# Two transformer blocks in one kernel: the hand-over from the first block's down projection to the linear attention of the second

## The reference, cut to what matters

```
x = x + rms_norm(f, norm_ffn_post_g)                      # f = (silu(h @ w_gate) * (h @ w_up)) @ w_down
mod = silu(c) @ w_ada + b_ada                             # sh1, sc1, g1, sh2, sc2, g2
h = rms_norm(x, norm1_g) * (1 + sc1) + sh1
gq, gk, gv, gr, glr, aq, ak, av = split(h @ w_in)         # 256, 256, 512, 512, 16, 512, 512, 512 columns
log_a = log_sigmoid(glr @ gla_w_gate + gla_b_gate) / 16
y_gla = gated linear attention of gq / 8, gk, gv, log_a   # then rms_norm, times silu(gr)
y_att = dilated attention of aq, ak, av
x = x + g1 * (concat(y_gla, y_att) @ w_out)               # then the second feed-forward
```

## Time and profile before

| | |
|---|---|
| time, median of 3 runs | 1385.92 us |
| profiled execution, its own time | 1384.31 us |
| its span, first to last instruction | 1382.6 us |
| TensorE busy | 1364.7 us |
| VectorE (DVE) busy | 873.8 us |
| ScalarE (ACT) busy | 584.9 us |
| GpSimd (POOL) busy | 57.4 us |
| mean granted clock of TensorE | 0.997 |
| DMA | 146.82 MB, 106 GB/s |

### The profile page before, as it was taken

One profiled execution on the slowest core, in us unless ns is written; L12 is line 12 of the kernel. 1 busy time (PEld: TensorE's weight loads), 2 busy tenths in 40 slices (PEclk: granted clock), 3 DMA queues, 4 the chain that ended last, 5 costly groups with the idle time before them and its releaser, 6 DMA issues.

```text
span 1382.6 us, 18985 instructions
## 1 busy us (share of the span) xinstructions
PE 1364.7 (99%) x6662; PEld 1113.0 (81%) x6662; DVE 873.8 (63%) x1473; ACT 584.9 (42%) x979; POOL 57.4 (4%) x119
## 2 busy tenths in 40 slices
PE   9999999999999999999998999999999999999999
PEld 7777777778988888888885787777798888888887
DVE  6667676678777777774336677776566656655221
ACT  5455455553453332233224534675455444443221
POOL 0000000000002121120000000000000000000000
PEclk9999999999999999999999999999999999999999
DMA  5222212214316555564431211111213232233332
GB/s 206 92 77 77 77 61 79 77 59 137 98 54 211 193 186 196 190 198 154 139 125 44 94 65 62 62 61 62 76 58 107 91 99 98 91 105 114 86 97 87
DMA packets 42615, 146.82 MB, mean 106 GB/s; under 512 B 5425, under 2 KB 5697, under 8 KB 42561
## 3 DMA queue, kind: packets, MB, share of 16 engines
q1 hardware_dynamic: 34592, 120.13, 26.7%
q0 software_dynamic: 7824, 25.70, 5.5%
q10 hardware_dynamic: 144, 0.26, 0.1%
HBM read 143.97 MB, written 2.10 MB: 106 GB/s over the span
## 4 chain that ended last, share of the span: by engine, by line
PE 92%; DVE 4%; ACT 3%; issue 1%; DMA 0%; DVEq 0%; SPq 0%; ACTq 0%
PE bank L644 61%; PE bank L846 13%; PE bank L662 4%; PE bank L785 3%; PE bank L872 2%; PE bank L962 2%; PE bank L893 1%; PE bank L911 1%; PE bank L752 1%; PE bank L1092 1%; PE bank L914 1%; DVE w_lo L1841 0%; DVE hbuf L1901 0%; ACT w_hi L1260 0%; DVE xT L2197 0%
## 5 line engine op out<-in xcount | busy, mean ns | idle before, releaser
L1841 DVE TENSOR_TENSOR w_lo<-raw,w_hi 128x1024 fp32r<-128x1024 f32 (+1 forms) x224 | 268.0, 1197 | 163.2 <-ACT w_hi L1260 158.3
L1260 ACT ACTIVATE w_hi<-raw 128x1024 fp32r<-128x1024 f32 (+1 forms) x224 | 231.6, 1035 | 285.9 <-PE bank L644 260.6
L644 PE MATMUL bank<-h_hi,w_hi 128*128 128x512 f32 x856 | 339.6, 397 | 0.7 <-DVE w_lo L1838 0.5
L644 PE MATMUL bank<-h_hi,w_lo 128*128 128x512 f32 x856 | 333.5, 390 | 0.0
L644 PE MATMUL bank<-h_lo,w_hi 128*128 128x512 f32 x856 | 333.3, 389 | 0.0
L644 PEld LDWEIGHTS bank<-h_hi,w_hi 128*128 128x128 f32 x856 | 160.7, 188 | 37.8 <-issue 3.8
L644 PEld LDWEIGHTS bank<-h_hi,w_lo 128*128 128x128 f32 x856 | 160.7, 188 | 34.0
L644 PEld LDWEIGHTS bank<-h_lo,w_hi 128*128 128x128 f32 x856 | 160.8, 188 | 33.8 <-issue 1.7
L644 PE MATMUL bank<-f_hi,w_lo 128*128 128x512 f32 x352 | 136.9, 389 | 0.0
L644 PE MATMUL bank<-f_hi,w_hi 128*128 128x512 f32 x352 | 136.9, 389 | 0.0
L644 PE MATMUL bank<-f_lo,w_hi 128*128 128x512 f32 x352 | 136.9, 389 | 0.0
(11 more groups left out here) (351 smaller groups left out, 1954.6 us busy)
## 6 DMA issues: line engine op xcount, KB each, us to landing
raw<-in_w_up SPq DMA_DIRECT2D x66, 512.0 KB, 3.3
ada<-in_w_ada POOLq DMA_DIRECT2D x96, 256.0 KB, 3.1
raw<-in_w_mix SPq DMA_DIRECT2D x47, 512.0 KB, 3.3
raw<-in_w_down SPq DMA_DIRECT2D x32, 512.0 KB, 3.5
raw<-in_w_in SPq DMA_DIRECT2D x25, 512.0 KB, 3.3
raw<-in_w_gate SPq DMA_DIRECT2D x22, 512.0 KB, 3.3
raw<-in_w_out SPq DMA_DIRECT2D x16, 512.0 KB, 3.3
raw<-in_w_down SPq DMA_DIRECT2D x16, 384.0 KB, 3.3
```

The lines of the kernel that those rows point to most:

```text
L644: last = pe.matmul(to[:, :], wt[:, slot, k, :], act_[:, rhs0 + k, :], start=(k == first and n == 0), stop=(k == K - 1 and n == 2))
L1260: act.activation(w_hi[:, s, k0:K, :], raw[:, s, k0:K, :], ACT.Copy).then_inc(hi_ready[s], 1)
L1841: dve.tensor_tensor(w_lo[:, s, k0:K, :], raw[:, s, k0:K, :], w_hi[:, s, k0:K, :].bitcast(F32), ALU.subtract).then_inc(split_ready[s], 1)
```

## The change

1. The masks are made in the down stage, behind the modulation of row 47, into a place in the space of h_lo (`masks_made`); SyncE copies them to `masks` by a DMA, and the sixth low part of x waits for it. GpSimd's two iotas no longer wait for `m2_free`.
2. The last down tiles are copied out with the gain of the post norm, the very last one is read from its bank. x is made by pairs of rows (`root_to`, `to_x`).
3. Tiles 0, 1 and 2 (into G1, G0, O0) take x * a as it is, without the second root and without the shift. Their products begin before the second root is known; `shift_products` makes the products of the shift with these tiles and with the rank columns (32 matmuls of one column), and root and shift are put on when they are copied out (`root_to_first`, `shifted`).
4. The rank tile is no unit any more: 32 padded columns, scaled by a (`wg_mod`), multiplied by x in four column groups of 32 (`rank_products`), and the gate product sums the four groups through four copies of the gate weights. w_in has one tile fewer.
5. The squares of x are made by pairs and summed on DVE, with one matmul of ones. The true h (root and shift) is made after that, for tiles 3 and on.
6. Levels and their tiles are moved by one: level 0 behind tile 5, level 7 behind the first two rows of the dilated tile. The key turn comes two rows later and is copied by ACT, ahead of the silu of gres. The gain on gres moves behind the state of chunk 0.

```diff
@@ TensorE
-            sum_squares_by_tile()
-            keep_clock(14)
-            two_units((S1, G1), (1, 0))
...
+            def shift_products():
+                pe.wait_ge(mod_sum[0], 25)
+                for kk in range(2):
+                    for j in range(4):
+                        k = 4 * kk + j
+                        pe.matmul(T1[32 * j:32 * j + 32, 3:4], wg_raw[:, k, :], modc[:, k:k + 1], start=(kk == 0), stop=(kk == 1))
+                for n, slot in (FIRST_TILES[2], FIRST_TILES[0], FIRST_TILES[1]):
+                    pe.wait_ge(split_ready[slot], w.next(split_ready[slot]))
+                    for k in range(KD):
+                        last = pe.matmul(T1[:, n:n + 1], raw[:, slot, k, :], modc[:, k:k + 1], start=(k == 0), stop=(k == KD - 1))
+                last.then_inc(shift_done, 1)
...
+            def rank_products():
+                for kk in range(2):
+                    for j in range(4):
+                        k = 4 * kk + j
+                        pe.matmul(S1[32 * j:32 * j + 32, :], wg_mod[:, k, :], xT[:, k, :], start=(kk == 0), stop=(kk == 1))
+            shift_products()
+            keep_clock(4)
+            third = 0
+            for k in range(KU):
+                pe.wait_ge(h_ready, w.next(h_ready))
+                first_step(0, k)
+                first_step(1, k)
+                for _ in range(FIRST_THIRDS[k]):      # (1, 1, 0, 1, 1, 1, 0, 0)
+                    first_step(2, third)
+                    third += 1
+            rank_products()
+            pe.wait_ge(x_sum, 2)
+            pe.matmul(S0[:, :], ones[:, :], x_sq_gla[:, 0, :], start=True, stop=True).then_inc(ms_ready, 1)
+            for k in range(third, KU):
+                first_step(2, k)
...
+            for k in range(KU):
+                pe.wait_ge(h_ready, w.next(h_ready))
+                unit(O1, gla_slot(3), h_hi, h_lo, k, k + 1)
+                if k == LAG:                          # 2
+                    pe.wait_ge(first_read, 1)
+                if k >= LAG:
+                    unit(S1, gla_slot(4), h_hi, h_lo, k - LAG, k - LAG + 1)
+                if k == Z_AT:                         # 2
+                    gate_products()
+            unit(S1, gla_slot(4), h_hi, h_lo, KU - LAG, KU)
...
+            project(0, 2)
+            level(7)
+            project(2, 4)
...
@@ ACT
+            for j in range(4):
+                unscaled_hi(2 * j)
+                unscaled_hi(2 * j + 1)
+                act.activation(x_sq_gla[:, 2 * j:2 * j + 2, :], xT[:, 2 * j:2 * j + 2, :], ACT.Square).then_inc(x_sq_r, 1)
+                if j == 0:
+                    act.wait_ge(shift_done, w.next(shift_done))
+                    act.activation(gshift[:, 0:2], T1[:, 0:2], ACT.Copy, scale=0.125)
+                    then(act.activation(gshift[:, 2:4], T1[:, 2:4], ACT.Copy))
...
+            act.wait_ge(kb_turned, w.next(kb_turned))
+            for t in range(2):
+                act.activation(kbt[:, t, :, :], TB[t][:, :].rearrange("p (c s) -> p c s", s=P), ACT.Copy).then_inc(kb_evac, 1)
@@ DVE, down stage, tile 7's place
                 add_squares(g)
                 modulation(46, 0)
                 modulation(47, 1)
+                make_masks()
@@ DVE, hand-over
-            post_norm(oT, lambda k: col("norm_ffn_post_g", k))
+            dve.tensor_tensor(wg_mod[:, :, :], wg_raw[:, :, :], mod_a[:, 0, :] ... , ALU.mult).then_inc(mod_sum[0], 1)
+            dve.wait_ge(unit_done[2], UNITS_BEFORE["gla"][2] + 1)
+            dve.memset(gacc[:, :, :], 0.0).then_inc(m2_free, 1)
             split_lo(2)
...
-            modulated_lo(0)
+            root_to(0, 1)
+            to_x(0, 1)
+            root_to(1, 1)
+            unscaled_lo(0)
+            to_x(1, 1)
+            root_to(2, 2)
+            unscaled_lo(1)
+            to_x(2, 2)
...
+            scaled_step(0)
+            scaled_step(1)
+            modulated_lo(0)
+            dve.tensor_tensor(glr[:, :], S1[:, :], rstd[:, :], ALU.mult).then_inc(first_read, 1)
+            scaled_step(2)
+            modulated_lo(1)
+            root_to_first(1)
+            for k in range(3, KD):
+                scaled_step(k)
+                modulated_lo(k - 1)
+            modulated_lo(KD - 1)
+            split_lo(gla_slot(5))
+            root_to_first(0)
+            root_to_first(2)
```

More of the change, by code:

```diff
@@ L733, in sum_squares @@
                 pe.matmul(S0[:, :], ones[:, :], sq[:, 1, :], start=False, stop=True).then_inc(ms_ready, 1)
[L735 to L755, removed]
             def project(k0, k1):
@@ new lines, in level @@
+            def level(lv):
+                pe.wait_ge(lev_ready, w.next(lev_ready))
+                for t in range(2):
+                    if lv >= 1:
+                        pe.wait_ge(lev_read, w.next(lev_read, times=2))
+                    for c in range(NCH):
+                        cc = slice(P * c, P * c + P)
+                        for m in range(2):
+                            half = slice(64 * m, 64 * m + 64)
+                            if lv == 0:
+                                last = pe.matmul(head_bank[2 * t + m][:, cc], gk[half, t, cc], gq[half, t, cc],
+                                                 start=True, stop=True)
+                            else:
+                                d = LEVELS[lv - 1]
+                                q_of = lev[half, lv % 2, t, cc].rearrange("p (b s) -> p b s", s=2 * d)[:, :, d:2 * d]
+                                last = pe.matmul(head_bank[2 * t + m][:, 64 * c:64 * c + 64].rearrange(
+                                    "p (b s) -> p b s", s=d), lev[half, lv % 2, t, cc], q_of, start=True, stop=True)
+                            if c == NCH - 1:
+                                last.then_inc(lev_done, 1)
@@ L1074, in _ @@
                     last.then_inc(gv_turned, 1)
[L1075 to L1095, removed]
-            pe.wait_ge(g_evac, w.next(g_evac, times=2))
-            project(0, 3)
+                if n == 5:
+                    pe.wait_ge(g_evac, 6)
+                level(n - 5)
+            pe.wait_ge(g_evac, 13)
+            project(0, 2)
+            level(7)
+            project(2, 4)
             pe.wait_ge(gv_evac, w.next(gv_evac, times=2))
-            pe.wait_ge(lev_read, w.next(lev_read, times=4))
             pe.wait_ge(lev_ready, w.next(lev_ready))
@@ L1127, in _ @@
                 last.then_inc(go_done, 1)
+                if c == 0:
+                    pe.wait_ge(kb_evac, w.next(kb_evac, times=2))
                 if c < NCH - 1:
@@ L1628, in _ @@
             act.preload_act_table_set("natural_log_exp_and_others")
[L1629 removed]
+            down(lambda g, c: out_tile(g, c, oT, OB, isinstance(c, int) and c == KD - 1))
+            split_hi(2)
             inverse_rms()
[L1631 to L1639 removed]
@@ new lines, in _ @@
+            modulated_hi(2)
+            split_hi(gla_slot(5))
+            modulated_hi(3)
+            modulated_hi(4)
+            shifted(1, 2)
+            modulated_hi(5)
+            act.wait_ge(z_done, w.next(z_done))
+            for t in range(2):
+                act.activation(zs[t][0], TB[t][:, :], ACT.Identity, bias=col("gla_b_gate_2", t)).then_inc(z_copied, 1)
+            modulated_hi(6)
+            modulated_hi(7)
+            act.wait_ge(z_copied, w.next(z_copied, times=2))
+            for t in range(2):
+                z, l = zs[t]
+                then(act.activation(l, z, ACT.Abs))
+                then(act.activation(l, l, ACT.Exp, scale=-1.0))
+                act.activation(l, l, ACT.Ln, bias=ones[:, 0:1]).then_inc(z_ln, 1)
@@ L2496, in _ @@
                     split_lo(2)
+                    dve.wait_ge(gres_r, w.next(gres_r))
+                    for h in range(4):
+                        last = dve.tensor_scalar(gres[:, h, :], gres[:, h, :], col("gla_norm_g_2"), None, ALU.mult)
+                    then(last)
                 if c == 1:
```

304 lines of the change are left out of this document (166 added, 138 removed).

## The result

The changed kernel takes 1391.13 us (median of 6 runs, 1390.67 to 1392.83), the kernel before 1385.82 (6 runs, 1384.02 to 1389.18): a ratio of 1.0044 with a 95% interval of 1.0034 to 1.0054. Forecast were 1380.2 us and a range that ended at 1387.5. The profiled execution took 1390.67, its span is 1389.0, 6.4 us more than before.

What follows compares the result with a forecast made beforehand. TensorE was taken as the bound, so time could come only from stretches without useful products: 7.7 us gained before level 0, less 1.0 around level 7 and 1.0 at the chunks, gives 5.7 and 1380.2 us; range 1376.5 to 1387.5.

Steps and rivals of the forecast that it cites:

- the stall at the masks: Last down tile: 4.95 us of masks on DVE delay the split of slot 2, so TensorE waits 2.4 us.
- the iotas on POOL: GpSimd, behind its last ada issue at 727.97: 0.5 us, counted as covered by more than 10 us.
- the clock of 1.00: Shift products on: one-column records over 7 us were expected at full clock; a clock of 0.5 at 748 meant wrong.
- five tiles and the gate products done: Second block, before level 0's products: five useful tiles and gate products done at 788.4, 7.7 us before 796.13.
- Rival 1: Half clock from the shift products on, possibly started by the mask stall: costs 5.0 us, total 1385.2; chance 0.34.
- the weight path is dense: Shift products: argument against half clock there, beside 2.0 us of idleness up to 857.4 that left the clock at 1.00.
- The shift products at 0.22 each: Behind the sum of squares: 32 one-column matmuls at 0.22 us, 7.0 in all, ending at 751.4.
- The waits at the second root: TensorE before the first three pairs of true h, near 771 to 777: waits of 1.9, 1.3 and 1.3 us.
- The rank products: Eight 512-column products in four column groups running together: 1.7 us, replacing a unit of 5.46.
- The estimate of 2.9: Rank products by the skill's 2.38 times for three column tiles: 2.9 us, making the result 1.2 later.
- The late losses: 1.0 us around level 7 (waits 1.6 and 1.4 against 2.0) and 1.0 before chunk 2 through ACT's later silu.
- the mark: 796.13 in the old kernel, the products of level 0, with five useful tiles and the rank tile done.

Runs made afterwards that it cites:

- e1: The changed kernel without the drain behind GpSimd's second iota, which raises const_ready itself: 1385.01 us, ratio 0.9998 to the kernel before.
- e7: The kernel before with part 1 of the change alone (masks behind row 47's modulation, iotas and drain behind the last ada load): 1395.40 us, ratio 1.0080.
- e11: The kernel before with part 1 alone, but iotas, drain and masks at the earlier places of e2: 1385.76 us, ratio 1.0005.
- e9: e3 plus tile 2's shift products behind its last product, keep-clock fillers around the second root, dilated tile's weight split behind the eighth factors' arguments: 1375.88 us, ratio 0.9936.
- e3: e2 with shift products that stream 64 equal columns instead of one: 1377.78 us, ratio 0.9943 to the kernel before.
- e2: The changed kernel with iotas and drain four modulation rows earlier and masks in the seventh down tile, where DVE idles: 1380.13 us, ratio 0.9964.
- e4: e2 with the key copies on DVE again and ACT making silu before them: 1380.57 us, ratio 0.9958 to the kernel before.
- e8: e9 with an extra GpSimd drain, tile 2's shift copied only after the gate products, and both distances behind chunk 1's state: 1375.60 us, ratio 0.9934.
- e10: e9 with both distances of the dilated pair behind the last state update, that of chunk 2: 1376.21 us, ratio 0.9933.

## Why the prediction was wrong

**The step that failed** is the stall at the masks, where the prediction put "the iotas on POOL (0.5, behind its last ada issue at 727.97)" among the covered work. Right were the 4.95 us of DVE and, without the drain, the 2.4 of stall (e1). Left out was the instruction between iotas and DVE, the drain of 7.98. It stood in the kernel's text, and its length in the trace of before; I had not asked for it, since no view of waits named it. Masks ready at 742.7 instead of 737.6 are 5.2 us more of stall: 7.6 instead of 2.4. e7 shows it as part 1's own, e1 and e11 as gone with the drain or the place. The second step that failed is the clock of 1.00 that the sum used throughout, behind the stall and in the one-column products; the runs showed 0.51 and 0.50 there.

**From the forecast to the trace.** From 736.17, where TensorE wants slot 2, to five tiles and the gate products done, the forecast has 52.2 us (788.4) and the trace 64.5 (806.54 less one tile's 24 products, 5.46, and its turn, 0.44: 800.6). The 12.2 are: stall 5.2; 18 products at half clock 3.2; shift products and keep-clock 9.1 instead of 8.0, 1.1; 63 products 15.14 instead of 14.3, 0.8; rank products to first true pair 0.3; from there 16.9 instead of 15.3, 1.6, which is what six products take at half clock over full (2.93 less 1.38 in e9). Against the same products at full clock (4.02 before, e3 and e9) the clock took 8.0 in all: 3.2 in the 18 products, 3.3 up to the end of the 63, 1.5 in the six. The eight shift products with 32-column weights gave 1.5 back: 0.24 together instead of 1.76. So the 12.2 are 5.2 for the drain and 8.0 for the clock, less 1.0 for all the rest.

**The clock.** Rival 1 had it, with a chance of 0.34, as one loss of 5 in the shift products; its remark that the stall can start it too came true as well, 3.2 more. From the shift products to the 63rd product it cost 3.3 in the changed kernel against e3: 6.96 instead of 5.50, keep-clock 1.92 instead of 0.95, first projections 15.14 instead of 14.31. In e2, without any stall, it was 3.2 (5.99, 1.92 and 16.06). In e1 it was nearly the 5: 7.93, 1.92 and 15.75, 4.8 in all. I held "the weight path is dense" against the rival; in e2 the loads of weights were as dense as in e3 (4.99 and 4.71 of 5.00), and the clock fell all the same with one column a product, and stayed with 64. Why e1 lost more than e2 stays open.

The Trainium skill says in TensorE: Matmul & The Clock Gate, PE-mode transpose, that a transpose does not count as busy in the same way. The one-column products behaved as if that held for them too: the clock fell to 0.51 while the engine was busy 1.00 of 1.00. The Trainium skill's page TensorEngine Tiling (Array Packing), Instruction Overhead, has a matmul of one column take as long as one of 60. The trace agrees, with 64: at full clock 29 records fill the 3 us from 743 to 746 in e2 and in e3.

**What held.** The shift products at 0.22 each: 6.96 for 24 tile products, 0.29 each with a part of them at half clock; e3 has 0.23 at full clock. Only the eight with 32-column weights were cheaper (0.24 together instead of 1.76). The rank products took 1.85 (forecast 1.7), 3.7 times faster than the 6.8 reckoned for one after the other. The estimate of 2.9 by the Trainium skill's 2.38 for three column tiles (TensorE: Matmul & The Clock Gate, Packing small matmuls) was too high for these four groups; the measurement decides. The waits at the second root were 1.8, 0.96 and 0.96 (1.9, 1.3, 1.3), with the pairs 1.92 apart as forecast (1.96).

**The late losses** came to 1.9 of span beyond the mark, as forecast (2.0): the waits 1.3 and 1.1 around level 7 (1.6 and 1.4; the old kernel waited 2.0 there) and 1.1 before chunk 2 (1.0). These waits make 1.5 of the 1.9. Of the last, the chain of the changed kernel runs as the prediction had it, through ACT's silu and squares, DVE's scaled output and one distance to the state. What the prediction did not see is that the gain on gres, which was to fit into the same wait, ends only 0.34 before ACT does, so that DVE's own queue would hold the state nearly as long (e4). Moving the distance, 1.5 on either path, let that wait go, and brought another (e8, e10).

**The size of the idea.** With masks and most of the clock's loss out of the way (e3) the change is 7.9 us faster than before; the forecast's 5.7 with its 2.4 of stall given back are 8.1. So close an agreement is partly luck: 1.5 lost to the clock after the second root and 1.5 gained in the products with 32-column weights cancel. The structure of the sum was sound; an unread instruction and a rival that was given too little weight turned its sign.

## What to carry to other kernels

Before moving a step, list every instruction in it on every engine, the sequencers' own too, and ask the trace for the length of each: a hidden drain shows up in no wait until it is moved to where someone waits. Price a stall together with the clock after it: here 7.6 us of stall cost another 3.2 in the 18 products behind it (1.7 in e7). Where small products must fill a gap, try them with more columns: here 64 instead of 1 cost no time, and the clock stayed at 2.4 GHz through them. Before taking a late engine off a path, look how long the next path is: in e4 it was as long.
